# Two halves of an expert table added in PSUM by two products of 128 columns a token; copied out by ScalarE and VectorE in turn

## The reference

```python
def peer(hn, w_q, subkeys, u, v):
    q = (xt @ w_q).reshape(T, H, 2, PEER_QDIM // 2)
    s = jnp.einsum('thcd,cnd->thcn', q, subkeys)
    s1, i1 = lax.top_k(s[:, :, 0], K)          # K = 16 of 128 keys, on each side
    s2, i2 = lax.top_k(s[:, :, 1], K)
    cand = (s1[..., :, None] + s2[..., None, :]).reshape(T, H, K * K)
    sc, ci = lax.top_k(cand, K)
    e1 = jnp.take_along_axis(i1, ci // K, axis=-1)
    e2 = jnp.take_along_axis(i2, ci % K, axis=-1)
    idx = e1 * PEER_NKEYS + e2                 # 16384 experts
    g = jax.nn.softmax(sc, axis=-1)
    ...
    a = jnp.einsum('cd,chkd->chk', xc, u[ic])
    act = (jax.nn.gelu(a.astype(jnp.float32)) * gc).astype(xc.dtype)
    return jnp.einsum('chk,chkd->cd', act, v[ic])
```

## Time and profile before

| | |
|---|---|
| runs | 4273.81 us median of 3 (4264.08 to 4284.89) |
| profiled execution, span from first to last instruction | 4269.6 us (its device time is not listed apart) |
| busy in the span: TensorE, VectorE, ScalarE | 4059.4, 2362.1, 1504.6 us |
| busy in the table stage, 1084.7 to 1536.4 us | 451.70, 427.21, 351.10 us |
| mean granted TensorE clock of the whole execution | 0.964 |
| table products (L705) | 512 |
| reductions (L685) | 128 |

### The profile page before, as it was taken

The page is one execution under the profiler, slowest core; times in us unless marked ns, Lnnn a source line. Parts: engine busy times, 40 slices in busy tenths (PEclk is TensorE's granted clock), DMA queues, the critical chain, the costliest instruction groups (busy, mean ns, idle before and its releaser), DMA issues. The chain is left out here.

```text
span 4269.6 us, 47277 instructions
## 1 busy us (share of the span) xinstructions
PE 4059.4 (95%) x18056; PEld 3239.5 (76%) x18056; DVE 2362.1 (55%) x4095; ACT 1504.6 (35%) x2600; POOL 85.6 (2%) x65
## 2 busy tenths in 40 slices
PE   8999999999999999999999998899998998998998
PEld 6667777788888878888887766777886766776886
DVE  3454445799899954544444356555434346565433
ACT  3222324233777742322222322333222232243221
POOL 0010000000000000000000001000000001000000
PEclk9988899999999999999999989999999989999999
DMA  3211113344555566666663222332332322242332
GB/s 125 77 60 30 38 40 116 100 141 133 165 205 190 177 245 196 190 193 188 189 195 101 85 69 70 95 125 84 94 90 74 97 60 72 77 148 74 94 89 69
DMA packets 183363, 497.15 MB, mean 116 GB/s; under 512 B 17826, under 2 KB 51268, under 8 KB 182116
## 3 DMA queue, kind: packets, MB, share of 16 engines
q1 hardware_dynamic: 183140, 494.14, 36.7%
HBM read 407.56 MB, written 85.98 MB: 116 GB/s over the span
## 5 line engine op out<-in xcount | busy, mean ns | idle before, releaser
L371 DVE TENSOR_TENSOR stream_lo<-stream_raw,stream_hi 128x1024 fp32r<-128x1024 f32 (+1 forms) x615 | 745.6, 1212 | 748.5 <-ACT stream_hi L363 747.1
L363 ACT ACTIVATE stream_hi<-stream_raw 128x1024 fp32r<-128x1024 f32 (+1 forms) x615 | 642.8, 1046 | 1430.5 <-PE experts_ps L847 492.0
L847 PE MATMUL experts_ps<-outputs_a_hi,stream_lo 128*128 128x512 f32 x1024 | 404.2, 395 | 0.0
L399 PE MATMUL experts_ps<-h_hi,stream_hi 128*128 128x512 f32 x1024 | 402.1, 393 | 1.5 <-PEq L100 1.5
L847 PE MATMUL experts_ps<-outputs_a_hi,stream_hi 128*128 128x512 f32 x1024 | 398.3, 389 | 4.2 <-DVE outputs_a_lo L818 4.2
L399 PE MATMUL experts_ps<-h_hi,stream_lo 128*128 128x512 f32 x1024 | 402.3, 393 | 0.0
L847 PE MATMUL experts_ps<-outputs_a_lo,stream_hi 128*128 128x512 f32 x1024 | 402.1, 393 | 0.0
L399 PE MATMUL experts_ps<-h_lo,stream_hi 128*128 128x512 f32 x1024 | 401.8, 392 | 0.0
L2334 PE MATMUL ffn_ps<-h_hi,stream_hi 128*128 128x512 f32 x704 | 287.4, 408 | 25.3 <-DVE h_lo L2371 25.3
L2334 PE MATMUL mid_ps<-h_hi,stream_hi 128*128 128x512 f32 x672 | 288.2, 429 | 24.0 <-DVE h_lo L2371 20.8
L2336 PE MATMUL ffn_ps<-h_hi,stream_lo 128*128 128x512 f32 x704 | 279.4, 397 | 0.0
(11 more groups left out here) (439 smaller groups left out, 7146.3 us busy)
## 6 DMA issues: line engine op xcount, KB each, us to landing
stream_raw<-u SPq DMA_DIRECT2D x128, 512.0 KB, 3.9
stream_raw<-v SPq DMA_DIRECT2D x128, 512.0 KB, 4.1
stream_raw<-l_gu SPq DMA_DIRECT2D x88, 512.0 KB, 3.5
expert_hidden<-experts_gelu SPq DMA_DIRECT2D x128, 256.0 KB, 4.2
expert_weights<-built SPq DMA_DIRECT2D x8, 4096.0 KB, 14.2
built<-expert_weights SPq DMA_DIRECT2D x32, 1024.0 KB, 7.8
built<-expert_hidden SPq DMA_DIRECT2D x128, 256.0 KB, 4.1
stream_raw<-l_gate SPq DMA_DIRECT2D x48, 512.0 KB, 3.9
```

The costliest lines, as they stand in the source:

```text
L363: self.nc.scalar.activation(self.hi[n % self.RING][:, 0:w], self.raw[n % self.RAW][:, 0:w], ACT.Copy).then_inc(self.hi_done, 1)
L371: self.nc.vector.tensor_tensor(self.lo[n % self.RING][:, 0:w], self.raw[n % self.RAW][:, 0:w], self.hi[n % self.RING][:, 0:w].bitcast(F32) ...
L399: mm = self.nc.tensor.matmul(self.ps[n % 2], a, b[:, k, :], start=(k == 0 and m == 0), stop=(k == DC - 1 and m == 2))
L847: mm = nc.tensor.matmul(ps[d], v, a[b % RING][:, :], start=(b == 0 and m == 0), stop=(b == KEYS - 1 and m == 2))
```

## The change

TensorE multiplies `hot1` twice for each token, by the high and by the low half of `hot2`, 128 columns each; the second product adds onto the first in PSUM. A quad then takes one bank, and six banks rotate in place of three pairs. What is taken out is a plain copy of 512 columns, by ScalarE for even quads and by VectorE for odd ones. On ScalarE the copy stands after gelu and the high part, ahead of the `ones` of the step. TensorE waits for the copy of six quads before, of whichever engine made it; SyncE waits for both engines before it stores a table; both copying engines wait for a table's buffer to be stored.

```diff
-    QUAD, RING, PLACES, BUILT = 4, 3, 3, 2
-    N = SEQ // QUAD
+    QUAD, RING, BUILT = 4, 3, 2
+    N, PLACES = SEQ // QUAD, len(banks)
...
         def place(quad):
-            return ps[:, 1024 * (quad % PLACES):1024 * (quad % PLACES) + 1024].rearrange("p (t s e) -> p t s e", t=QUAD, s=2)
+            return banks[quad % PLACES].rearrange("p (t e) -> p t e", t=QUAD)
+
+        def home(quad):
+            tt, at = quad // TILE, quad % TILE * QUAD
+            return built[tt % BUILT][:, :, at:at + QUAD].rearrange("p e t -> p t e")
+
+        def wait_home(eng, quad):
+            tt = quad // TILE
+            if tt >= BUILT and quad % TILE < 2:
+                eng.wait_ge(stored[tt % BUILT], 16 * (tt // BUILT))
...
+                def take(quad):
+                    wait_home(act, quad)
+                    act.wait_ge(mm_done, quad + 1)
+                    nc.scalar.activation(home(quad), place(quad), ACT.Copy).then_inc(taken_s, 1)
+
                 for n in range(first, last):
                     hidden.activate(act, n - 1)
                     chunks.high(act, E0 + n + AHEAD)
+                    for quad in quads(n - 1):
+                        if quad % 2 == 0:
+                            take(quad)
                     for quad in quads(n):
                         ones(quad)
...
                 def take(quad):
-                    tt, at = quad // TILE, quad % TILE * QUAD
-                    if tt >= BUILT and quad % TILE == 0:
-                        dve.wait_ge(stored[tt % BUILT], 16 * (tt // BUILT))
+                    wait_home(dve, quad)
                     dve.wait_ge(mm_done, quad + 1)
-                    V.tensor_reduce(built[tt % BUILT][:, :, at:at + QUAD].rearrange("p e t -> p t e"),
-                                    place(quad).rearrange("p t s e -> p t e s"), AX_X, ALU.add).then_inc(taken, 1)
+                    V.tensor_copy(home(quad), place(quad)).then_inc(taken_v, 1)
 
                 for n in range(first, last):
                     for quad in quads(n - 1):
-                        take(quad)
+                        if quad % 2 == 1:
+                            take(quad)
...
                         if quad >= PLACES:
-                            pe.wait_ge(taken, quad - PLACES + 1)
+                            before = quad - PLACES
+                            pe.wait_ge(taken_v if before % 2 else taken_s, before // 2 + 1)
                         for k in range(QUAD):
-                            mm = nc.tensor.matmul(place(quad)[:, k, :, :], hot1[quad % RING][:, k, :], hot2[quad % RING][:, k, :, :],
-                                                  start=True, stop=True)
+                            for part in range(2):
+                                mm = nc.tensor.matmul(place(quad)[:, k, :], hot1[quad % RING][:, k, :], hot2[quad % RING][:, k, part, :],
+                                                      start=(part == 0), stop=(part == 1))
                         mm.then_inc(mm_done, 1)
...
-                            sp.wait_ge(taken, quad + 1)
+                            sp.wait_ge(taken_s, (tt + 1) * TILE // 2)
+                            sp.wait_ge(taken_v, (tt + 1) * TILE // 2)
```

More of the change, by code:

```diff
@@ L606, in _, with expert_weights @@
                 keep(TT - 1)
-def expert_weights(nc, name, C, chosen, w_dram, chunks, hidden, ps, built, weighing):
-    QUAD, RING, PLACES, BUILT = 4, 3, 3, 2
-    N = SEQ // QUAD
+def expert_weights(nc, name, C, chosen, w_dram, chunks, hidden, banks, built, weighing):
+    QUAD, RING, BUILT = 4, 3, 2
+    N, PLACES = SEQ // QUAD, len(banks)
     TILE = WT // QUAD
@@ L621, in expert_weights @@
         hot2 = [st.sb(f"hot2_{b}", [P, QUAD, 2, KEYS], F32R) for b in range(RING)]
-        minus_done, g_hi_done, g_lo_done, far_done, hot1_done, hot2_done, mm_done, taken = (
-            st.sem(x) for x in ("minus_done", "g_hi_done", "g_lo_done", "far_done", "hot1_done", "hot2_done", "mm_done", "taken"))
+        minus_done, g_hi_done, g_lo_done, far_done, hot1_done, hot2_done, mm_done, taken_s, taken_v = (
+            st.sem(x) for x in ("minus_done", "g_hi_done", "g_lo_done", "far_done", "hot1_done", "hot2_done", "mm_done",
+                                "taken_s", "taken_v"))
         stored = [st.sem(f"stored{b}") for b in range(BUILT)]
@@ L2327, in expert_part @@
                 weighing = Weighing(st, built[0], w_dram, a_dram, hidden)
-                expert_weights(nc, "weights", C, chosen, w_dram, chunks, hidden, ps[:, 1024:4096], built, weighing)
+                expert_weights(nc, "weights", C, chosen, w_dram, chunks, hidden, bank[2:8], built, weighing)
             expert_outputs(nc, "outputs", x, w_dram, a_dram, chunks, weighing, bank, C2, A["positions"], constants2)
```

## The result

The changed kernel takes 4318.06 us (median of 4 runs, 4317.66 to 4322.76) against 4268.94 for the kernel before (4 runs, 4262.66 to 4284.89). The ratio is 1.0111, 95% interval 1.0092 to 1.013: slower by 49 us, where +54 us and 4328 us had been forecast. Its profiled execution took 4318.14 us, with a span of 4316.4.

A forecast was written before the change was run, and what follows sets the result against it. TensorE was taken to bound the table stage, packed with products and waiting for nobody. Products +54 us, VectorE's relief worth nothing and ScalarE's copies zero, on a median of 4273.8, gave 4328 us, range 4272 to 4346.

The forecast's parts named there:

- TensorE sets the pace of the stage: From first to last table product, TensorE is busy for all 451.70 us and waits for nobody; VectorE's margin is 25 us.
- A load holds a 128-column product to 0.112 us: Table products on TensorE: 128 columns can't hide their weight load, so 1,024 products cost 114.7 us, against 60.8 before.
- the two rows: Full-fp32 trace rows: sixteen products of 128 columns with loads 0.112 us apart, eight of one column 0.111 apart.
- term of +54 us: Table products in the stage: 1,024 at 0.112 us make 114.7, less 60.8 for the 512 before.
- Adding up in PSUM costs nothing: Table products: two adding into the same 128 columns one after the other add no time.
- The copies: Table copies out of PSUM: 64 on ScalarE at 0.60 us (38 us), 64 on VectorE at 691 ns (44 us).
- Nothing is exposed on ScalarE: ScalarE's copies ahead of the `ones` don't delay TensorE; tightest margin about 0.2 to 0.3 us, cost zero.
- the rule of 0.4 us for each of eight steps: With 1.2 us copies, steps after a single even quad would lose some 0.4 us each: 3 us.
- Rival 2: Table products: loads short enough for 128 columns to stream at 0.064 us a product; +4.5 us, 4278; chance 0.12.
- rival 3: Table products: few columns served at the full-fp32 rate, 0.223 us a product; +168 us, 4442; chance 0.12.
- Rival 4: ScalarE's copies stretch and `ones` come late: 10 to 40 us on top of load-bound products, 4338 to 4370; chance 0.04.
- Rival 5: VectorE was the hidden bound of the stage and its relief outweighs the products; 4265; chance 0.04.

The follow-up runs named there:

- e1: Kernel before with each 256-column table product split into two of 128 columns, VectorE still adding the halves, no new copies: 4326.6 us, ratio 1.0131.
- e6: Changed kernel with all 128 copies on VectorE, none on ScalarE: 4326.93 us, ratio 1.0132.
- e7: Changed kernel with the copies written to a contiguous place instead of one column in every 64: 4325.19 us, ratio 1.0122.
- e3: Kernel before with one 128-column product a token (high half only), VectorE copying instead of reducing: 4268.11 us, ratio 0.9992.
- e4: Changed kernel with its 1,024 products cut to 64 columns each, halves side by side, no accumulation: 4322.65 us, ratio 1.0129.
- e8: Kernel before with its one product a token cut from 256 to 192 columns, VectorE copying the high half alone: 4268.32 us, ratio 0.9992.
- e5: Changed kernel with hot1 and hot2 in bf16 in place of fp32r, same 1,024 products: 4275.57 us, ratio 1.0008.
- e2: Changed kernel with one 256-column product a token put back; ScalarE and VectorE copy out the high half only: 4276.84 us, ratio 1.002.
- e9: Changed kernel with bf16 tables and all copies on VectorE, none on ScalarE: 4274.88 us, ratio 1.0004.
- e10: Kernel before with bf16 tables, one 256-column product a token and VectorE's reduction kept: 4269.06 us, ratio 0.999.

## Why the prediction was right, point by point

- **TensorE sets the pace of the stage.** Right. It is busy in all of the 505.2 us and waits for nobody, and e1, e6 and e7, which move 20 to 90 us of work on VectorE and ScalarE, leave the stage at 505.1.
- **A load holds a 128-column product to 0.112 us.** Right, though the two rows were misread in one point. A full-fp32 product leaves two records, each with a load of its own, as the prediction says elsewhere. So the sixteen and eight of the earlier trace rows are records, of eight and of four products (L1287 is written for four), and 0.111 us is the price of a load with its pass, not of a full-fp32 product. An fp32r product has one load and one record (1,024 of each at L724), so the sum holds.

  Of the two rows only the earlier trace rows shows the load: two full-fp32 records of 512 columns at L1036, 0.59 us long each and 1.02 together, stand 0.43 us apart, which makes 0.107 for 128 columns, so the earlier trace rows could have come from its columns too.

  The further eight products of a group cost 0.111 us each, as each load of the earlier trace rows. The forecast of 1.79 us for sixteen met 1.80, that of 0.90 for eight met 0.91. The term of +54 us measured 54.0 in the stage. That it is the load and not the columns, e3, e4 and e8 show for fp32r: with 64, 128 and 192 columns a product costs the same. e5 shows that a bf16 load is not held to it.

```profile
3523.11 1.02 PE L1036 MATMUL mid_ps<-gla_sq,stream_const 128*128 128x512 f32 x2
```

- **Adding up in PSUM costs nothing.** Right (e1).
- **The copies.** Mis-sized: 0.60 and 0.69 us were taken, 1.09 and 1.08 measured, because I took rows with a contiguous target although the reduction's row with the strided target stood as the other end. e7 settles that the stride is the cause. VectorE was therefore 343 us busy in place of about 315, and ScalarE waited 89 us for expert products in place of 110. The Trainium skill (SBUF — State Buffer, section "Door 1: The DMA port swizzle") says that an access which crosses to a new 16-byte line pays a penalty; the copies, each of whose elements goes to a new line, agree with it by 1.08 against 0.69 us. No run tries another stride, so that the line is the reason isn't shown.
- **Nothing is exposed on ScalarE.** Right in the result, wrong in the working. I had both tables wanted when the group begins. The second quad's table is wanted only after the first quad's products, 0.48 us later in the kernel before and 0.9 in the changed one, so margins are larger by that. With the products put back (e2) even copies of 1.09 us cost 1.3 us in the stage, where the rule of 0.4 us for each of eight steps gave 3.
- **The total.** 4328 forecast, 4318.06 measured. The stage came out as forecast. Of the 10 us that are missing, 5 are in the runs of before themselves (4273.8 at the time of the forecast, 4268.9 beside the changed kernel). The other 5 are outside the stage; the profiled executions differ by 8 us in the part ahead of the expert stages, which has nothing to do with the change, but that the medians differ for that reason isn't shown. The same products gave 1.0131 in e1 and 1.0132 in e6, medians 56 and 54 us above those of before.
- **The rivals.** Rival 2 had a shorter load than full fp32's, rival 3 full fp32's two loads and passes for few columns. The group of sixteen rules both out, 1.80 us where they had 1.02 and 3.6, and e3 rules out rival 2 once more: half the columns saved 3.2 us and not 28. Rival 4 needed copies well over 1.2 us; they took 1.09. Rival 5 is ruled out by e2: 83 us less work on VectorE, and the stage 1.3 us longer.

## What to carry to other kernels

Where TensorE has no waits, count its weight loads beside its columns: split products, each with its own load, cost about the larger of the load and the columns. For fp32r tables of 128 columns a load was 0.111 us here, nearly the 0.12 us of a whole product of 256 columns. What shortened it was bf16 tables, at the price of bits. Relief for an engine that the bounding engine doesn't wait for turns into waiting, however many microseconds it is. When the cost of a copy is looked up in a neighbouring row, the stride of its target has to match as well as its shape.

## What the hardware showed that was not expected

- A copy of 512 fp32 columns out of PSUM took 1.08 us on VectorE and 1.09 on ScalarE with one element in every 256 bytes of the target, and 0.69 and 0.59 with a contiguous target: both engines are held to much the same 2 ns an element.
- Groups of bf16 table products had 0.27 us of idle time of the weight loads in front of them, in 72 of 72 groups (19.4 us in e5, e9 and e10), which stays unexplained. In the groups of fp32r products it is 5.9 to 6.0 us in all, 0.08 each. TensorE's products are busy all the while.
- In e5 the profile put 8.6 us of these waits down to ScalarE. With ScalarE's copies taken away (e9) they were still there: the engine named is the one that came last, not always the one to blame.
- The same untouched first part of the kernel took 784.5 to 792.5 us in two executions. Of the 6 us between e2's median and that of before, 1.3 are in the changed stage; the stage's own window tells that, and the ratio can't.
